# Split-precision products: one 512-column matmul for both activation halves in place of two of 256 columns

## The reference, cut to what matters

```python
x = x + 0.5 * swiglu_ffn(rms_norm(x, g1), w_gate1, w_up1, w_down1)        # 2048 -> 5632 -> 2048
h = rms_norm(x, mix_g)
u = h @ w_in                                    # convolution, q and kv latents, k rope, two gates
y_conv = conformer_conv_branch(u_conv, ...)     # GLU, 31-tap depthwise, LayerNorm, silu, 2048x2048
y_mla = mla_branch(c_q_raw, c_kv_raw, k_rope_raw, ...)                    # 16 heads, then 2048x2048
x = x + (sigmoid(gl_conv) * y_conv + sigmoid(gl_mla) * y_mla) @ w_out
x = x + 0.5 * swiglu_ffn(rms_norm(x, g2), w_gate2, w_up2, w_down2)
return rms_norm(x, g3)
```

## Time and profile before

| what | value |
|---|---|
| device time, median of 3 runs | 2488.96 us (2488.76 to 2491.82) |
| span of the profiled execution | 2489.8 us |
| PE busy, DVE busy, ACT busy | 2411.5, 1627.8, 1127.2 us |
| matmuls and weight loads on record | 19734 each |
| DMA | 430 MB, 173 GB/s, queue busy 51.9% |

### The profile page before, as it was taken

The page is one execution under the profiler, slowest core; times in us unless marked ns, Lnnn a source line. Parts: engine busy times, 40 slices in busy tenths (PEclk is TensorE's granted clock), DMA queues, the critical chain, the costliest instruction groups (busy, mean ns, idle before and its releaser), DMA issues.

```text
span 2489.8 us, 51907 instructions
## 1 busy us (share of the span) xinstructions
PE 2411.5 (97%) x19734; PEld 2379.9 (96%) x19734; DVE 1627.8 (65%) x2441; ACT 1127.2 (45%) x1227; POOL 16.2 (1%) x12
## 2 busy tenths in 40 slices
PE   6999999999999999989999998999999999999997
PEld 6999999999999999977799998999999999999997
DVE  6655556565555778799967777677555555554444
ACT  5555554543334454345443355334555455543332
POOL 2000000000000000000000000000000000000000
PEclk9999999999999999999999999999999999999998
DMA  5555555565554555422255545555555555565552
GB/s 194 185 180 183 182 181 185 180 206 186 185 185 154 179 187 181 160 91 97 92 170 185 179 159 160 185 184 177 179 185 180 182 185 178 185 201 187 185 186 102
DMA packets 111215, 430.03 MB, mean 173 GB/s; under 512 B 12609, under 2 KB 12738, under 8 KB 111170
## 3 DMA queue, kind: packets, MB, share of 16 engines
q1 hardware_dynamic: 111170, 429.43, 51.9%
HBM read 427.29 MB, written 2.10 MB: 172 GB/s over the span
## 4 chain that ended last, share of the span: by engine, by line
PE 88%; DVE 8%; issue 2%; ACT 2%; DVEq 0%; DMA 0%; ACTq 0%; SPq 0%
PE bank L556 29%; PE bank L554 29%; PE bank L555 29%; DVE conv_acc L958 2%; DVE w_lo L780 2%; ACT w_hi L332 1%; DVE h L872 1%; DVE row_inv L1029 0%; DVE tree L1119 0%; ACT probs L401 0%; PE scores L688 0%; DVE x L1204 0%; PE misc L679 0%; PE misc L614 0%; DVE padded L1136 0%
## 5 line engine op out<-in xcount | busy, mean ns | idle before, releaser
L780 DVE TENSOR_TENSOR w_lo<-raw,w_hi 128x1024 fp32r<-128x1024 f32 (+2 forms) x760 | 985.1, 1297 | 785.1 <-ACT w_hi L332 773.2
L332 ACT ACTIVATE w_hi<-raw 128x1024 fp32r<-128x1024 f32 (+2 forms) x760 | 846.9, 1115 | 1179.3 <-PE bank L556 1170.4
L554 PE MATMUL bank<-h,w_hi 128*128 128x256 f32 x4032 | 1145.4, 284 | 29.8 <-DVE h L872 23.1
L555 PE MATMUL bank<-h,w_hi 128*128 128x256 f32 x4032 | 1143.0, 283 | 0.0
L556 PE MATMUL bank<-h,w_lo 128*128 128x256 f32 x4032 | 1142.9, 283 | 0.0
L554 PEld LDWEIGHTS bank<-h,w_hi 128*128 128x128 f32 x4032 | 776.1, 192 | 32.0 <-issue 24.3
L555 PEld LDWEIGHTS bank<-h,w_hi 128*128 128x128 f32 x4032 | 776.1, 192 | 0.2
L556 PEld LDWEIGHTS bank<-h,w_lo 128*128 128x128 f32 x4032 | 776.1, 192 | 0.0
L556 PE MATMUL bank<-hidden,w_lo 128*128 128x256 f32 x1408 | 395.6, 281 | 0.0
L554 PE MATMUL bank<-hidden,w_hi 128*128 128x256 f32 x1408 | 394.2, 280 | 0.0
L555 PE MATMUL bank<-hidden,w_hi 128*128 128x256 f32 x1408 | 391.4, 278 | 0.0
(11 more groups left out here) (163 smaller groups left out, 1632.1 us busy)
## 6 DMA issues: line engine op xcount, KB each, us to landing
raw<-in_ffn_up SPq DMA_DIRECT2D x352, 512.0 KB, 3.3
raw<-in_ffn_down SPq DMA_DIRECT2D x128, 704.0 KB, 4.0
raw<-in_conv_in SPq DMA_DIRECT2D x64, 512.0 KB, 3.3
raw<-in_mla_out SPq DMA_DIRECT2D x64, 512.0 KB, 3.4
raw<-in_conv_gate SPq DMA_DIRECT2D x32, 512.0 KB, 3.7
raw<-in_conv_out SPq DMA_DIRECT2D x32, 512.0 KB, 3.3
raw<-in_w_out SPq DMA_DIRECT2D x32, 512.0 KB, 3.3
raw<-in_latents SPq DMA_DIRECT2D x24, 512.0 KB, 3.5
```

The source lines that it names most:

```text
L332: act.activation(w_hi[:, j, 0:n], raw[:, j, 0:n], ACT.Copy).then_inc(hi_ready, 1)
L554: pe.matmul(dst[:, 0:T], w_hi[:, j, rows], moving[:, 0:T], start=start, stop=False)
L555: pe.matmul(dst[:, 0:T], w_hi[:, j, rows], moving[:, T:2 * T], start=False, stop=False)
L780: dve.tensor_tensor(w_lo[:, j, 0:n], raw[:, j, 0:n], w_hi[:, j, 0:n], ALU.subtract).then_inc(lo_ready, 1)
```

## The change

Every product becomes two matmuls. w_hi takes all 512 columns of the moving tile in one matmul and writes all 512 columns of the bank; w_lo takes the rounded part and accumulates into columns 0 to T. The first product of a tile runs w_hi first, since it starts the bank, and all others run w_lo first. The sum of the two halves of the bank moves to DVE: each of the 372 evictions becomes a copy of columns T to 2T to SBUF (`half`), an addition of columns 0 to T to it, and then the multiplication by the factor (or the residual step), each waiting for the one before. `tile_read` is counted up by the last of the three. The value tiles, the scores and the rotation keep their matmuls. The two semaphores `half_copied` and `half_added` count through all evictions; `s0` of a stage is the number of them before it.

```diff
             def multiply(j, at, dst, moving, start, stop):
                 rows = slice(at * P, (at + 1) * P)
-                pe.matmul(dst[:, 0:T], w_hi[:, j, rows], moving[:, 0:T], start=start, stop=False)
-                pe.matmul(dst[:, 0:T], w_hi[:, j, rows], moving[:, T:2 * T], start=False, stop=False)
-                return pe.matmul(dst[:, 0:T], w_lo[:, j, rows], moving[:, 0:T], start=False, stop=stop)
+                def by_hi():
+                    return pe.matmul(dst[:, 0:2 * T], w_hi[:, j, rows], moving[:, 0:2 * T], start=start, stop=stop)
+                def by_lo():
+                    return pe.matmul(dst[:, 0:T], w_lo[:, j, rows], moving[:, 0:T], start=False, stop=False,
+                                     skip_group_check=True)
+                if start:
+                    by_hi()
+                    return by_lo()
+                by_lo()
+                return by_hi()
...
-            def times(dst, src, factor, tile, complete):
+            def join(dst, src, joined, complete):
                 dve.wait_ge(*complete)
-                dve.tensor_tensor(dst, src[:, 0:T], factor, ALU.mult).then_inc(tile_read, 1)
+                dve.tensor_copy(half[:, :], src[:, T:2 * T]).then_inc(half_copied, 1)
+                dve.wait_ge(half_copied, joined + 1)
+                dve.tensor_tensor(dst, src[:, 0:T], half[:, :], ALU.add).then_inc(half_added, 1)
+                dve.wait_ge(half_added, joined + 1)
+
+            def times(dst, src, factor, tile, complete, joined=None):
+                join(dst, src, joined, complete)
+                dve.tensor_tensor(dst, dst, factor, ALU.mult).then_inc(tile_read, 1)
                 dve.wait_ge(tile_read, tile + 1)
...
-                    dve.wait_ge(*after_unit(phase, g, 3 if tiles == 1 else 2 * part + 1))
-                    dve.scalar_tensor_tensor(out=x[:, m, :], in0=b[:, 0:T], scalar=factor, in1=x[:, m, :],
+                    join(prod[:, :], b, m + phase.s0, after_unit(phase, g, 3 if tiles == 1 else 2 * part + 1))
+                    dve.scalar_tensor_tensor(out=x[:, m, :], in0=prod[:, :], scalar=factor, in1=x[:, m, :],
                                              op0=ALU.mult, op1=ALU.add).then_inc(tile_read, 1)
```

More of the change, by code:

```diff
@@ L67, with __init__ @@
 class Phase:
-    def __init__(self, name, n, sizes, g0, t0):
-        self.name, self.n, self.sizes, self.g0, self.t0 = name, n, sizes, g0, t0
+    def __init__(self, name, n, sizes, g0, t0, s0):
+        self.name, self.n, self.sizes, self.g0, self.t0, self.s0 = name, n, sizes, g0, t0, s0
 def plan():
-    out, group, tile = [], 0, 0
+    out, group, tile, joined = [], 0, 0, 0
     for name, n, sizes, tiles in PHASES:
-        out.append(Phase(name, n, sizes, group, tile))
+        out.append(Phase(name, n, sizes, group, tile, joined))
         group += n
         tile += n * tiles
+        joined += n * (5 if name == "heads" else tiles)
     return out
@@ L114, in encoder @@
         prod = sb("prod", [P, T])
+        half = sb("half", [P, T])
         ta = sb("ta", [P, T])
@@ L186, in encoder @@
         tile_read = sem("tile_read")
+        half_copied = sem("half_copied")
+        half_added = sem("half_added")
         x_loaded = [sem(f"x_loaded{n}") for n in range(4)]
@@ L879, in work @@
                     if part == 0:
-                        times(ta[:, :], bank[0], rstd[:, :], g * 2 + phase.t0, after_unit(phase, g, 1))
+                        times(ta[:, :], bank[0], rstd[:, :], g * 2 + phase.t0, after_unit(phase, g, 1),
+                              g * 2 + phase.s0)
                         return
-                    times(tc[:, :], bank[1], rstd[:, :], g * 2 + (phase.t0 + 1), after_unit(phase, g, 3))
+                    times(tc[:, :], bank[1], rstd[:, :], g * 2 + (phase.t0 + 1), after_unit(phase, g, 3),
+                          g * 2 + (phase.s0 + 1))
                     dve.wait_ge(gate_active, g + (before + 1))
@@ L995, in latent @@
                 times(tc[:, :], bank[tile % 2], rstd[:, :], latents.t0 + tile,
-                      after_unit(latents, tile // 2, 2 * (tile % 2) + 1))
+                      after_unit(latents, tile // 2, 2 * (tile % 2) + 1), latents.s0 + tile)
                 absorb(KT + n, tc[:, :], g_col, dst, square=False)
@@ L1004, in latents_work @@
                     dst = td if part else tc
-                    times(dst[:, :], bank[part], rstd[:, :], latents.t0 + tile, after_unit(latents, g, 2 * part + 1))
+                    times(dst[:, :], bank[part], rstd[:, :], latents.t0 + tile, after_unit(latents, g, 2 * part + 1),
+                          latents.s0 + tile)
                     linked(dve.tensor_tensor(dst[:, :], dst[:, :], (sin if part else cos), ALU.mult))
@@ L1047, in head_pair @@
                 t0 = g * 6 + heads.t0
+                s0 = g * 5 + heads.s0
                 first = isinstance(g, int) and g == 0
@@ L1086, in mla_out_work @@
                 if part == 0:
-                    times(ta[:, :], bank[0], rstd[:, :], g * 2 + phase.t0, after_unit(phase, g, 1))
+                    times(ta[:, :], bank[0], rstd[:, :], g * 2 + phase.t0, after_unit(phase, g, 1),
+                              g * 2 + phase.s0)
                     return
                 dve.wait_ge(mla_open, g + 1)
-                times(merged32[:, g, 0:T], bank[1], tb[:, :], g * 2 + (phase.t0 + 1), after_unit(phase, g, 3))
+                times(merged32[:, g, 0:T], bank[1], tb[:, :], g * 2 + (phase.t0 + 1), after_unit(phase, g, 3),
+                      g * 2 + (phase.s0 + 1))
             def mla_out_mid(g, r, i):
@@ L1112, in conv_gate_work @@
                     dve.wait_ge(conv_open, m - 1)
-                times((ta, tb)[part][:, :], bank[part], rstd[:, :], m + gates.t0, after_unit(gates, g, 2 * part + 1))
+                times((ta, tb)[part][:, :], bank[part], rstd[:, :], m + gates.t0, after_unit(gates, g, 2 * part + 1),
+                      m + gates.s0)
             def add_up(src, before):
@@ L1184, in conv_out_work @@
                 times(tb[:, :], bank[part], merged32[:, m, T:2 * T], m + phase.t0,
-                      after_unit(phase, g, 2 * part + 1))
+                      after_unit(phase, g, 2 * part + 1), m + phase.s0)
                 dve.tensor_tensor(tc[:, :], tb[:, :], merged32[:, m, 0:T], ALU.add).then_inc(merge_step, 1)
```

10 lines of the change are left out of this document (5 added, 5 removed).

## The result

The changed kernel takes 2512.82 us (median of 4 runs, 2510.9 to 2514.51) against 2488.86 for the one before in the same session (4 runs): 0.92% slower, ratio 1.0092, 95% interval 1.0079 to 1.0104. The forecast was 2413, with a range of 2385 to 2483.

The account below looks back on a forecast made before the run. PE was taken to bound some 5700 of 6416 products, DVE heads, neither conv_gate. 67.6 + 26.8 + 10.8 + 7 + 8 + 1.5 - 34 - 9 - 3 = 75.7 us off 2488.96 gave 2413, range 2385 to 2483.

Parts of the forecast that it names:

- the first term of PE's side: Merged w_hi matmul on PE: 216 ns assumed, a product 0.336 us in place of 0.360; up stages save 67.6 us.
- the fp32 row: Trace row of eight plain fp32 matmuls on PE, 512 cycles each, 0.216 us from start to start.
- The bounds, 213 and 240: Limits for the 512-column w_hi matmul on PE: 512 columns at 2.4 GHz, or twice 120 ns.
- rival 2: On PE each load costs its matmul 11 to 13 ns: w_hi 229 ns, product 0.349 us, time 2483; chance 0.12.
- The first reading: On PE the stream ends after about 109 ns, then waits for the next weight load, needing 118 to 120 ns.
- The third, a rate limit: On PE fp32r streams no faster than 256 columns in 120 ns; w_hi 240 ns, time 2537; chance 0.13.
- The second reading: On PE each matmul with a load beside it pays 11 to 13 ns extra.
- the right rival: The forecast's rival 2, a cost per weight load on PE: time 2483, chance 0.12.
- DVE's terms: Evictions on DVE: 0.85 us more each, 316 us in all; heads lose 34, conv_gate 9, up and down stages nothing.
- The point of decision: On PE, a w_hi matmul above about 232 ns means 5700 products save under 48 us, 8.4 ns each.
- rivals that put the w_hi matmul at 229 or more: On PE: the rate limit, w_hi 240 ns, chance 0.13, and the cost per load, 229 ns, chance 0.12.

Follow-up runs that it names:

- experiments 1 to 3: Changed kernel plus quiet tails of matmuls on PE alone, other engines done; 512 columns took 0.227 us in fp32r, 0.216 in bf16, 0.216 a pass in plain fp32.
- DVE's part alone: Against the kernel before: three matmuls a product kept, evictions in three operations with the same result; 2550.11 us, ratio 1.0246.
- PE's part alone: Against the kernel before: products as changed, evictions kept at one operation, omitting w_hi times the activations' low half; 2451.44 us, ratio 0.9849.

## Why the prediction was wrong

**The step that failed** is the first term of PE's side: "I take 216, the fp32 row, as the nearest in cycles". The 512-column matmul measured 236 ns on average in the up stages (227 to 241) and 229 in the down stages. The plain fp32 row was nearest in cycles, but it is not the same type, and experiments 1 to 3 show that the type matters: fp32r pays 13.4 ns beyond its stream where plain fp32 and bf16 pay 2 to 3. In the up stages a product saves 7 ns and not 24: of the 17 that are missing, 11 are this charge as a uniform run shows it (227 against 216) and 6 come with the alternation (353 against 347). The bounds, 213 and 240, held the average of every stage, though 229 of the 850 w_hi starts between 200 and 500 us are 241 ns apart; the value between them was the mistake. It makes 75 of the 96 us between the forecast and the measured span; conv_in and mla_out make 16 and latents 5.

**Which reading was right.** Nearest was the second, a charge of 11 to 13 ns per matmul with its load, rival 2 at 0.12. Its price was 229 ns (measured 227 in a uniform run, 229 in the down stages) and its time 2483, 30 us too low. Two terms of it were off. It had 11 ns a product in the up stages, and alternation raises the charge there, so that 6 to 7 are left: 13 us of the 30. And it had 8 us in conv_in and mla_out and nothing in latents, where DVE gave +0.6 and +3.7: 12 us. The first reading, the load as the bound at 256 columns, was wrong: the load is the bound only at 111 ns, below what 256 columns cost. The third, a rate limit, was wrong though the totals look like it (two short ones 240, one long 236). The second reading holds as a size, not as a fixed price of every load: half the load's columns don't halve the charge, and bf16 and plain fp32 load as well and hardly pay.

**The argument against the right rival.** The transposes' loads, 0.105 us each, and the ports of their own in the Trainium skill's page "SBUF — State Buffer" (section "A bandwidth-pool intuition that's wrong (but worth ruling out)") were weighed against it. Neither spoke to the point: the transposes run on plain fp32, and a load of 0.105 us doesn't exclude a charge of 13 ns. Whether ports are shared no run shows; the charge is there with all other engines quiet. The 2.5 ns of the Trainium skill's page "TensorE: Matmul & The Clock Gate" (section "Wait — 56ns, not 53.3ns?") hold for bf16 here (0.216 and 0.109 us) and for plain fp32, and not for fp32r.

**What was right.** DVE's terms: 0.85 us an eviction (0.91 measured), heads +34 (+34.2, and +33 in DVE's part alone), conv_gate +9 (+10.1), the up and down stages covered. DVE busy 1940.9 against "near 1930" (its own 316 us more would have made 1944).

**Smaller misses.** conv_in and mla_out were to gain 15, at 11.2 and 11.3 us a group; they measured 11.6 and 11.8. PE's part alone gave them 7 (3.7 and 3.0), DVE's part alone cost 2 and 4, so with the small saving DVE and PE nearly cancel. Latents were to gain 1.5 and lost 3.7: in PE's part alone it gained 1.2 and not 4.6, and in DVE's part alone it lost 5.6 and not 3.

**The point of decision.** The text had a w_hi matmul above 232 ns as slower than before; in the up stages it is 236 on average, and the kernel is slower. The chances did not follow from that: 0.25 lay on rivals that put the w_hi matmul at 229 or more, while no row had shown fp32r beyond 256 columns, the one thing that decides.

## What to carry to other kernels

Take a matmul's cost from a row of the same operand type: the charge beyond the stream was 13.4 ns a matmul for fp32r and 2.5 for bf16 and plain fp32, at 256 to 512 columns, so merging two fp32r matmuls saves about that charge and no more, and here the alternation of long and short took half of it back (7 ns saved a product). A change that moves work from PE to DVE belongs only in the stages where PE alone is the bound: there it gave 0.9% (1.5% with the long and the short matmuls of the up stages in runs), and everywhere it cost 0.9%. Before such a change is put in, a quiet tail of 48 matmuls of the new shape at the end of the kernel tells its price, if it has them in the kernel's order.

## What was not expected of the hardware

- fp32r, full clock, 128-column loads, same tiles throughout: 227, 174, 147 and 120 ns for 512, 384, 320 and 256 columns, N / 2.4 GHz plus 13.4 ns. 448 columns take 203. Below, the load bounds: 111 for 128 and for 192.
- At half clock the charge is not seen: 213 ns for 256 columns.
- The charge depends on tile and neighbours, 7 to 23 ns on average: with `hidden` moving 233 and 117 ns in uniform runs but 229 and 118 alternating; with `h` 227 and 120 uniform but 236 and 117 alternating, and 349 for the two together in pairs or runs of eight. What sets it is open. Half the rows, another bank and w_lo in place of w_hi leave it at 227.
- Narrower loads lower it at 256 columns (120 to 113 ns) and raise it at 512 (227 to 230 with 64 columns, 232 with 32).
- A stretch of 3.4 us at half clock falls at the start of a stage in some kernels and not in others with the same wait before it (4.0 us ahead of ffn2_up, 2.7 ahead of conv_in), and costs 1.7 us.
- A DVE copy of 128 x 256 fp32 from PSUM takes 0.42 us, no less than an operation with two inputs.
